# A two-layer attention and conv-FFN decoder on one core: side work of the attention stage placed anew, and four-head score banks lowered by VectorE

## The chip, the core and the metric

The kernel runs on one core of a Trainium2 chip. The metric is the device time of one execution in microseconds. The core has five instruction queues that run beside each other and meet at semaphores: TensorE (PE in the profile), VectorE (DVE), ScalarE (ACT), GpSimd (POOL) and SyncE (SP), which here issues DMAs only. Each queue runs its instructions in the order written; a waiting instruction holds up everything behind it on its engine.

## The reference

A trunk of two layers over 512 tokens of width 1024. In each layer a mixer (8 retention heads, 8 NSA heads in two key groups of four) is followed by a conv FFN, each between RMS norms. What the change touches is in the NSA heads:

```python
def nsa(nq, nkv, ngate, ...):
    kc, vc = compress(kv[0], ...), compress(kv[1], ...)      # 31 compressed keys and values
    def block(b):                                            # 128 queries at a time
        pc = masked_softmax(qb @ kc, mc)                     # compressed branch
        o_cmp = pc @ vc
        kg, vg = ks_blk[.., sel], vs_blk[.., sel]            # all 8 blocks are selected at 512 tokens
        ps = masked_softmax(qb @ kg, causal)                 # selected branch
        pwin = masked_softmax(qb @ kw, window and causal)    # window branch
        return g0 * o_cmp + g1 * (ps @ vg) + g2 * (pwin @ vw)
```

With 512 tokens and 8 blocks of 64 the selection takes every block and the window of 512 is the causal mask, so both branches are plain causal softmaxes over different keys. `masked_softmax` is exp(s - max) over its sum. The retention heads give the first half of the mixer's output `y`, the NSA heads the second; `w_out` multiplies both.

## The kernel before

Nearly all products are done in float32 accuracy from fp32r parts: a tensor `a` is held as `a_hi` (rounded) and `a_lo = a - a_hi`, and a product is three matmuls (hi·hi, hi·lo, lo·hi). Weights stream through a ring of six slots in 110 chunks per layer; ScalarE makes `w_hi` and GpSimd `w_lo`. The order of every engine is written out by hand, engine by engine, with counted semaphores.

The attention stage of a layer, around which the change is made, is a loop over 48 **items** `k`. The 16 **units** (query tile i, key group g, branch b) are softmaxes of 128 queries by 128·(i+1) keys for four heads; each unit has i+1 items, and each pair of units one more item for the compressed branch. For item k the engines do:

- PE: four transposes of the probabilities into a PSUM bank (`turn_p`, L1654; L1648 for the compressed branch), then the product of item k-2 with the values (`product`, L1677 and L1678), then side work by tables: score banks ("jobs") of later units (`SCORES_AT`, L1557 to L1563), one eighth of the last query projection f7 (`Q7_AT`, L1388), the compressed scores of group 1 (`CMP_AT`, L1577, L1583), transposes of the retention output (`turn_y` at `Y_AT`, L1595), and parts of the output projection (`WO_AT`, L1616).
- ACT: the transposed bank to `pt_h` (`p_round`, L839), then the exponentials of the jobs of item k-1 (`exps`, L813), and copies for side work.
- DVE: `pt_l` (`p_rest`, L926), then the minimum of each job's bank (`minima`, L1190; queries are negated, so a minimum is a maximum), and the rests of side work. `turn_p(k)` waits for `p_rest(k-2)` (semaphore `ptl`).
- POOL: the reciprocal of each sum (L603) and the scaling of the probabilities by it and the gate (L609).

A unit of query tile 0 (n = 6, 7, 14, 15) needs only 128 columns per head, so all four heads share one bank: one job, one minimum over four heads (128x4), but four exponentials of 128 columns, each with its own bias and with its sum accumulated. Two projections are spread over this stage too: f6 before the loop, f7 in it. `queries_first(f)` (ACT, two copies, L767) and `queries_rest(f)` (DVE, two instructions, L1135) take the projection out of its bank into `QS`. Bank 7 is shared: the compressed scores of group 0, then f7, then outputs. `compressed_first(g)` (DVE, L1210 to L1214) takes the compressed scores out and counts `c_step` to 3; f7's first matmul waits for that. `y_round(n)` (DVE) takes transposed retention output to `act_hi` (L1199) and `act_lo` (L926).

## Time and profile before

| | us |
|---|---|
| median of 3 runs | 1399.81 (1399.09 to 1399.86) |
| the profiled execution | 1401.01 |
| its span | 1399.1 |
| PE busy | 1363.3 (97%) |
| DVE / POOL / ACT busy | 713.3 (51%) / 700.1 (50%) / 606.3 (43%) |
| mean granted PE clock | 0.99 |

Matmuls are pipelined, so a PE that reads as busy can still be slow: when the granted clock is 0.5, PE is busy all the time and does half the work. The attention loop of layer 0 lies between about 200 and 310 us, that of layer 1 between about 890 and 1000 us.

### The profile page before, as it was taken

How to read it: one execution, taken by the hardware profiler on the slowest of the kernel's cores; microseconds unless marked ns; L12 is line 12 of the kernel's file. 1: busy time of each engine (PE TensorE's matmuls, PEld its weight loads, DVE VectorE, ACT ScalarE, POOL GpSimd, SP SyncE). 2: the span in 40 equal slices, each digit the busy share in tenths (PEclk: the TensorE clock that was granted, in tenths of full speed). 3: DMA queues.
4: the chain of work that ended last, by engine and by line, in shares of the span. 5: the costliest groups of instructions: out<-in, count | busy, mean ns of one | idle time of the engine just before them, and what ended most of it. 6: DMA issues, size and time to landing. Idle time of an engine off the chain costs nothing.

```text
span 1399.1 us, 17721 instructions
## 1 busy us (share of the span) xinstructions
PE 1363.3 (97%) x6904; PEld 1122.8 (80%) x6904; DVE 713.3 (51%) x900; ACT 606.3 (43%) x1087; POOL 700.1 (50%) x544
## 2 busy tenths in 40 slices
PE   8999988999999999999999999989999999999998
PEld 5889866778888888888888887767788888888886
DVE  5406556745544544644462075566355445556443
ACT  4233565756434333433442336656454333343322
POOL 2544775745444444544464456757435444445441
PEclk9999998999999999999999999989999999999999
DMA  5433420022333333333233333100323333333231
GB/s 202 136 100 106 131 65 16 1 91 91 105 91 97 99 93 103 90 103 93 61 121 112 108 106 119 31 16 2 121 68 115 104 91 104 93 96 100 90 106 61
DMA packets 34883, 127.19 MB, mean 91 GB/s; under 512 B 3952, under 2 KB 4464, under 8 KB 34416
## 3 DMA queue, kind: packets, MB, share of 16 engines
q1 hardware_dynamic: 34656, 125.53, 29.2%
q8 instruction: 56, 0.92, 0.3%
q10 hardware_dynamic: 144, 0.52, 0.1%
q14 instruction: 27, 0.22, 0.1%
HBM read 123.94 MB, written 2.10 MB: 90 GB/s over the span
## 4 chain that ended last, share of the span: by engine, by line
PE 89%; ACT 5%; DVE 3%; issue 1%; POOL 1%; DMA 0%; DVEq 0%; POOLq 0%; ACTq 0%; SPq 0%
PE bank L1719 33%; PE bank L1372 17%; PE bank L1751 17%; PE bank L1388 5%; PE bank L1616 3%; PE bank L1654 2%; PE bank L1677 2%; PE bank L1678 1%; ACT E L813 1%; PE bank L1562 1%; PE bank L1563 1%; PE bank L1476 1%; PE bank L1583 1%; PE bank L1340 1%; POOL w_lo L546 1%
## 5 line engine op out<-in xcount | busy, mean ns | idle before, releaser
L546 POOL TENSOR_TENSOR w_lo<-raw,w_hi 128x1024 fp32r<-128x1024 f32 x216 | 521.3, 2419 | 468.4 <-ACT w_hi L643 468.1
L643 ACT ACTIVATE w_hi<-raw 128x1024 fp32r<-128x1024 f32 x220 | 230.9, 1054 | 241.9 <-DMA raw<-wstream 241.8
L1719 PE MATMUL bank<-act_hi,w_hi 128*128 128x512 f32 (+1 forms) x768 | 286.0, 372 | 0.6 <-DVE act_lo L926 0.6
L1719 PE MATMUL bank<-act_hi,w_lo 128*128 128x512 f32 (+1 forms) x768 | 285.2, 371 | 0.0
L1719 PE MATMUL bank<-act_lo,w_hi 128*128 128x512 f32 (+1 forms) x768 | 285.2, 371 | 0.0
L885 ACT ACTIVATE cv<-bank,par 128x512 f32<-128x512 f32 x88 | 68.6, 779 | 286.0 <-PE bank L1719 286.0
L1301 DVE SCALAR_TENSOR_TENSOR cv<-bank,par,cv 128x511 f32<-128x511 f32 x88 | 66.0, 750 | 225.3 <-ACT cv L885 225.3
L1719 PEld LDWEIGHTS bank<-act_hi,w_hi 128*128 128x128 f32 x768 | 144.7, 188 | 26.9 <-DVE act_lo L926 1.6
L1719 PEld LDWEIGHTS bank<-act_hi,w_lo 128*128 128x128 f32 x768 | 144.7, 188 | 25.2
L1719 PEld LDWEIGHTS bank<-act_lo,w_hi 128*128 128x128 f32 x768 | 144.7, 188 | 24.7
L1372 PE MATMUL bank<-w_hi,act_hi 128*128 128x512 f32 (+1 forms) x384 | 144.5, 376 | 0.6 <-DVE w_lo L926 0.5
L1372 PE MATMUL bank<-w_lo,act_hi 128*128 128x512 f32 (+1 forms) x384 | 143.5, 374 | 0.0
L1372 PE MATMUL bank<-w_hi,act_lo 128*128 128x512 f32 (+1 forms) x384 | 143.1, 373 | 0.0
L926 DVE TENSOR_TENSOR act_lo<-gff,act_hi 128x512 fp32r<-128x512 f32 x40 | 92.9, 2334 | 88.0 <-ACT act_hi L896 88.0
L1751 PE MATMUL bank<-w_hi,act_hi 128*128 128x512 f32 x320 | 124.7, 390 | 0.0
L1751 PE MATMUL bank<-w_hi,act_lo 128*128 128x512 f32 x320 | 124.5, 389 | 0.0
L1751 PE MATMUL bank<-w_lo,act_hi 128*128 128x512 f32 x320 | 124.5, 389 | 0.0
L926 DVE TENSOR_TENSOR pt_l<-bank,pt_h 128x512 fp32r<-128x512 f32 (+1 forms) x96 | 65.8, 687 | 76.1 <-ACT pt_h L839 75.8
L1310 DVE TENSOR_TENSOR gff<-cv 128x512 f32<-128x512 f32 x44 | 101.7, 2312 | 4.3 <-ACT cv L891 2.9
L839 ACT ACTIVATE pt_h<-bank 128x512 fp32r<-128x512 f32 (+1 forms) x96 | 56.8, 594 | 78.6 <-PE bank L1678 78.3
L1372 PEld LDWEIGHTS bank<-w_hi,act_hi 128*128 128x128 f32 x384 | 72.1, 188 | 14.4 <-DVE w_lo L926 1.3
L1372 PEld LDWEIGHTS bank<-w_hi,act_lo 128*128 128x128 f32 x384 | 72.2, 188 | 12.6
(175 smaller groups left out, 2231.9 us busy)
## 6 DMA issues: line engine op xcount, KB each, us to landing
raw<-wstream SPq DMA_DIRECT2D x220, 512.0 KB, 3.6
g_all<-gains SPq DMA_DIRECT2D x2, 2048.0 KB, 7.0
x_out<-x SPq DMA_DIRECT2D x8, 256.0 KB, 2.0
x<-x_in SPq DMA_DIRECT2D x3, 512.0 KB, 9.3
const<-consts SPq DMA_DIRECT2D x1, 1030.0 KB, 13.7
g_all<-gains ACTq DMA_DIRECT2D x1, 512.0 KB, 5.1
x<-x_in SPq DMA_DIRECT2D x2, 256.0 KB, 5.2
par<-pars SPq DMA_DIRECT2D x2, 235.0 KB, 3.5
```

The source lines that it names most:

```text
L546: nc.gpsimd.tensor_tensor(w_lo[:, s, :], raw_slot(s), r32(w_hi[:, s, :]), ALU.subtract)\
L643: nc.scalar.activation(w_hi[:, s, :], raw_slot(s), ACT.Copy).then_inc(hi_ready, 1)
L839: nc.scalar.activation(pt_h[0:rows, k % 2, :], bank[0:rows, PT_BANK(k), :], ACT.Copy)\
L885: nc.scalar.activation(cv[:, p, s, :], bank[:, u, :], ACT.Identity, bias=w2[:, col:col + 1, 3], scale=w2[:, col:col + 1, 2])\
L926: return nc.vector.tensor_tensor(out, a, b, ALU.subtract)
L1301: nc.vector.scalar_tensor_tensor(out=y[:, 1:SEQ], in0=u[:, 0:SEQ - 1], scalar=taps[:, col:col + 1, 1], in1=y[:, 1:SEQ], op0=ALU.mult, op1= ...
L1310: nc.vector.tensor_tensor(gff[:, it * 2 + p, :], cv[:, p, 0, :], cv[:, p, 1, :], ALU.mult).then_inc(g_ready, 1)
L1372: last = mm(bank[:, b0 + t, 0:width], a, b, start=(k == 0 and n == 0), stop=(k == KD - 1 and n == 2))
L1388: last = mm(bank[:, F_BANK[f], :], a, v, start=(k == 0 and n == 0), stop=(k == KD - 1 and n == 2))
L1616: last = mm(bank[:, t, :], a, b, start=(k == 0 and n == 0), stop=(k == KD - 1 and n == 2))
L1719: last = mm(bank[:, b, first:end], a, v, start=(k == 0 and n == 0), stop=(k == KD - 1 and n == 2), skip_group_check=True)
L1751: last = mm(bank[:, t + 4 * half, :], a, b, start=(k == 0 and n == 0), stop=(k == TAIL_K[-1] and n == 2))
```

## The change

Three things are done, the same in both layers.

1. The compressed scores of group 0 go one projection step earlier (steps 11 to 14 in place of 12 to 15), and `compressed_first(0)` stands behind the minimum of job 13 in place of after the loop. f6 leaves its bank at item 1 in place of inside the early loop; f7 runs at items 0 to 6 (in place of 1 to 8) and leaves its bank at item 7 (in place of 9). `turn_y` goes to items 8, 11, 14, 17, its first waits for f6 only (`q_l` 6 in place of 8), and its `act_hi` copy goes from DVE to ACT. Jobs, the group-1 compressed scores, two chunk splits and the output projection move by one to three items.
2. For the four units with one bank (`LOWERED`), DVE subtracts the minimum from the bank into `E`, ACT takes one exponential of 128x512 in place, and DVE sums it (`sums`, two items behind the job).
3. POOL's reciprocal of these units waits for `summed` in place of `e_done`.

The diff (lines of context cut):

```diff
@@ -290,6 +290,7 @@
+        UNITS = [(i, g, b) for g in range(NKV) for i in reversed(range(T)) for b in range(2)]
@@ -307,6 +308,9 @@
         e_done = sem("e_done", G * NU)
+        LOWERED = [n for n in range(NU) if UNITS[n][0] == 0]
+        lowered = sem("lowered", len(LOWERED))
+        summed = sem("summed", len(LOWERED))
@@ -333,19 +337,19 @@
         HALF_0_FIRST, HALF_0 = (0, 3, 2, 1), (3, 2, 1, 0)
-        CMP_BANK, CMP_AT = (7, 0), (0, 22)
-        Q7_AT = 1
-        Y_AT = (9, 11, 13, 15)
-        WO_AT = {24: [(0, 0)], 26: [(0, 1)], 28: [(3, 0)], 31: [(3, 1)], 36: [(2, 0)], 37: [(2, 1)], 38: [(3, 2)],
-         39: [(3, 3)], 41: [(1, 0)], 43: [(1, 1)], 44: [(2, 2)], 47: [(2, 3)]}
+        CMP_BANK, CMP_AT = (7, 0), (0, 24)
+        Q7_AT = {0: (0, 1), 1: (1, 3), 2: (3, 4), 3: (4, 5), 4: (5, 6), 5: (6, 7), 6: (7, KD)}
+        Q6_END, Q7_END = 1, 7
+        Y_AT = (8, 11, 14, 17)
+        WO_AT = {27: [(0, 0)], 28: [(0, 1)], 31: [(3, 0)], 32: [(3, 1)], 38: [(2, 0)], 39: [(2, 1)], 40: [(3, 2)],
+         41: [(3, 3)], 42: [(1, 0)], 43: [(1, 1)], 44: [(2, 2)], 47: [(2, 3)]}
...
-        WO_CHUNK_AT = {1: C_WO + 1, 8: C_WO + 2, 17: C_WO + 3, 27: C_WO + 4, 33: C_WO + 5}
...
-
-        UNITS = [(i, g, b) for g in range(NKV) for i in reversed(range(T)) for b in range(2)]
+        WO_CHUNK_AT = {3: C_WO + 1, 10: C_WO + 2, 17: C_WO + 3, 27: C_WO + 4, 33: C_WO + 5}
@@ -374,8 +378,8 @@
-        UNIT_SCORES = {4: (3, 4), 5: (5, 6), 6: (7,), 7: (10,), 8: (11, 12, 13, 14), 9: (15, 16, 17, 18),
-               10: (19, 20, 21, 22), 11: (23, 24, 25, 26), 12: (28, 30), 13: (32, 34), 14: (36,), 15: (38,)}
+        UNIT_SCORES = {4: (3, 4), 5: (5, 6), 6: (7,), 7: (10,), 8: (12, 13, 14, 16), 9: (17, 18, 19, 20),
+               10: (21, 22, 23, 24), 11: (25, 26, 27, 28), 12: (29, 31), 13: (33, 35), 14: (37,), 15: (39,)}
@@ -599,7 +603,10 @@
                 pool.wait_ge(p_scaled, upto(p_scaled, l, scaled_through(n - SB, 2 * p + 1)))
-            pool.wait_ge(e_done, upto(e_done, l, EXP_NO[n, 2 * p + 1]))
+            if n in LOWERED:
+                pool.wait_ge(summed, upto(summed, l, LOWERED.index(n) + 1))
+            else:
+                pool.wait_ge(e_done, upto(e_done, l, EXP_NO[n, 2 * p + 1]))
@@ -801,6 +808,11 @@
             width = P * (UNITS[n][0] + 1)
+            if n in LOWERED:
+                act.wait_ge(lowered, upto(lowered, l, LOWERED.index(n) + 1))
+                e = E[:, slot, :, col:col + width]
+                nc.scalar.activation(e, e, ACT.Exp, scale=-1.0).then_inc(e_done, G)
+                return
@@ -813,6 +825,11 @@
+
+        def y_round(n):
+            act.wait_ge(y_turned, upto(y_turned, l, n + 1))
+            nc.scalar.activation(act_hi[:, 0:4, n * P:(n + 1) * P],
+                                 bank[:, 0, :].rearrange("p (k c) -> p k c", k=4), ACT.Copy).then_inc(y_h, 1)
@@ -826,8 +843,6 @@
                 hi(l, C_WO)
-            if z == 13:
-                queries_first(6)
@@ -862,8 +877,12 @@
                 exps(z)
-            if k == Q7_AT + 8:
+            if k == Q6_END:
+                queries_first(6)
+            if k == Q7_END:
                 queries_first(7)
+            if k in Y_AT:
+                y_round(Y_AT.index(k))
@@ -1191,13 +1210,26 @@
                 .then_inc(m_step, 1)
+            if n in LOWERED:
+                slot, col = E_AT[n]
+                dve.wait_ge(m_step, upto(m_step, l, z + 1))
+                dve.wait_ge(pt_done, upto(pt_done, l, last_turn(E_AFTER[n]) + 1))
+                nc.vector.tensor_tensor(E[:, slot, :, col:col + width],
+                                        bank[:, S_BANK(z), :].rearrange("p (q c) -> p q c", q=G),
+                                        s_bias[:, n % SB, :].unsqueeze(2).broadcast_to([P, G, width]),
+                                        ALU.subtract).then_inc(lowered, 1)
+
+        def sums(n):
+            slot, col = E_AT[n]
+            dve.wait_ge(e_done, upto(e_done, l, EXP_NO[n, G - 1]))
+            if n >= SB:
+                dve.wait_ge(rec_done, upto(rec_done, l, PAIR_NO[n - SB, 1] + 1))
+            nc.vector.tensor_reduce(out=s_sum[:, n % SB, :], in_=E[:, slot, :, col:col + P], axis=AXX,
+                                    op=ALU.add).then_inc(summed, 1)
...
-        def y_round(n):
-            dve.wait_ge(y_turned, upto(y_turned, l, n + 1))
-            nc.vector.tensor_copy(act_hi[:, 0:4, n * P:(n + 1) * P],
-                                  bank[:, 0, :].rearrange("p (k c) -> p k c", k=4)).then_inc(y_h, 1)
+        def y_rest(n):
@@ -1222,9 +1254,8 @@
                 compressed_values_rest()
-            if z == 14:
-                queries_rest(6)
-        compressed_first(0)
+            if z == 13:
+                compressed_first(0)
@@ -1275,10 +1306,15 @@
                 minima(z)
-            if k == Q7_AT + 8:
+            for z in jobs_at(k - 2):
+                if JOBS[z][0] in LOWERED:
+                    sums(JOBS[z][0])
+            if k == Q6_END:
+                queries_rest(6)
+            if k == Q7_END:
...
             if k - 1 in Y_AT:
-                y_round(Y_AT.index(k - 1))
+                y_rest(Y_AT.index(k - 1))
@@ -1588,7 +1624,7 @@
                 pe.wait_ge(y_step, upto(y_step, l, 8))
-                pe.wait_ge(q_l, upto(q_l, l, 8))
+                pe.wait_ge(q_l, upto(q_l, l, 6))
@@ -1631,8 +1667,8 @@
                 second_layer()
-            if n >= 12:
-                compressed_scores(0, n - 12)
+            if 11 <= n < 15:
+                compressed_scores(0, n - 11)
@@ -1683,10 +1719,10 @@
                 job_scores(z)
-            if Q7_AT <= k < Q7_AT + KD:
-                if k == Q7_AT:
+            if k in Q7_AT:
+                if k == min(Q7_AT):
                     pe.wait_ge(c_step, upto(c_step, l, 3))
-                feature_tile(l, 7, range(k - Q7_AT, k - Q7_AT + 1))
+                feature_tile(l, 7, range(*Q7_AT[k]))
```

On **VectorE**, just ahead of the attention loop of layer 0. `s_bias<-bank` is the minimum of a score bank, `c_stat` and `cE<-bank` are `compressed_first(0)`, `QS` is `queries_rest(6)`, `pt_l` belongs to items 0 to 2. Before:

```order
L1190 TENSOR_REDUCE s_bias<-bank 128x1 [waits s_done] x6
L1135 SCALAR_TENSOR_TENSOR QS<-bank,QS 64x512 [waits q_h]
L1135 SCALAR_TENSOR_TENSOR QS<-bank,QS 64x512
L1190 TENSOR_REDUCE s_bias<-bank 128x1 [waits s_done]
L1210 TENSOR_REDUCE c_stat<-bank 128x16 [waits cs_done]
L1212 TENSOR_SCALAR c_stat<-c_stat 128x16 [waits c_step]
L1214 TENSOR_TENSOR cE<-bank,c_stat 128x512 [waits c_step]
L926 TENSOR_TENSOR pt_l<-bank,pt_h 128x512 [waits pth] x3
```

After:

```order
L1209 TENSOR_REDUCE s_bias<-bank 128x1 [waits s_done] x5
L1242 TENSOR_REDUCE c_stat<-bank 128x16 [waits cs_done]
L1244 TENSOR_SCALAR c_stat<-c_stat 128x16 [waits c_step]
L1246 TENSOR_TENSOR cE<-bank,c_stat 128x512 [waits c_step]
L1209 TENSOR_REDUCE s_bias<-bank 128x1 [waits s_done] x2
L945 TENSOR_TENSOR pt_l<-bank,pt_h 128x512 [waits pth] x2
L1154 SCALAR_TENSOR_TENSOR QS<-bank,QS 64x512 [waits q_h]
L1154 SCALAR_TENSOR_TENSOR QS<-bank,QS 64x512
L945 TENSOR_TENSOR pt_l<-bank,pt_h 128x512 [waits pth]
```

The compressed scores' three instructions now stand ahead of two minima and of f6's rest, and f6's rest stands behind the `pt_l` of items 0 and 1.

On **ScalarE**, around items 7 to 10 of layer 0. `E,s_sum` are exponentials with their sums, `E<-E` the new single exponential, `QS` is `queries_first(7)`, `act_hi<-bank` the moved copy of `turn_y`, `w_hi` a weight chunk. Before:

```order
L839 ACTIVATE pt_h<-bank 32x512 [waits pv_done,pt_done]
L813 ACTIVATE E,s_sum<-bank,s_bias 128x128 [waits pt_done,m_step]
L813 ACTIVATE E,s_sum<-bank,s_bias 128x128 x3
L839 ACTIVATE pt_h<-bank 128x512 [waits pv_done,pt_done]
L767 ACTIVATE QS<-bank 64x512 [waits w_used]
L767 ACTIVATE QS<-bank 64x512
L839 ACTIVATE pt_h<-bank 128x512 [waits pv_done,pt_done] x2
L813 ACTIVATE E,s_sum<-bank,s_bias 128x128 [waits pt_done,m_step]
L813 ACTIVATE E,s_sum<-bank,s_bias 128x128 x3
L846 ACTIVATE o_a<-bank 64x512 [waits pv_done]
```

After:

```order
L774 ACTIVATE QS<-bank 64x512 [waits w_used]
L774 ACTIVATE QS<-bank 64x512
L854 ACTIVATE pt_h<-bank 32x512 [waits pv_done,pt_done]
L814 ACTIVATE E<-E 128x4x128 [waits lowered]
L831 ACTIVATE act_hi<-bank 128x4x128 [waits y_turned]
L650 ACTIVATE w_hi<-raw 128x1024 [waits raw_loaded2]
L854 ACTIVATE pt_h<-bank 128x512 [waits pv_done,pt_done] x3
L814 ACTIVATE E<-E 128x4x128 [waits lowered]
L831 ACTIVATE act_hi<-bank 128x4x128 [waits y_turned]
L861 ACTIVATE o_a<-bank 64x512 [waits pv_done]
```

f7's copies now stand ahead of the `pt_h` of item 8; four exponentials have become one, which waits for `lowered`; and two `act_hi` copies have joined the queue.

On **VectorE**, items 7 to 11 of layer 0 (`QS` is `queries_rest(7)`, `E<-bank` the lowering, `s_sum<-E` the sum, `act_lo` the rest of `turn_y`). Before:

```order
L1190 TENSOR_REDUCE s_bias<-bank 128x4 [waits s_done]
L926 TENSOR_TENSOR pt_l<-bank,pt_h 32x512 [waits pth]
L926 TENSOR_TENSOR pt_l<-bank,pt_h 128x512 [waits pth]
L1135 SCALAR_TENSOR_TENSOR QS<-bank,QS 64x512 [waits q_h]
L1135 SCALAR_TENSOR_TENSOR QS<-bank,QS 64x512
L926 TENSOR_TENSOR pt_l<-bank,pt_h 128x512 [waits pth]
L1190 TENSOR_REDUCE s_bias<-bank 128x4 [waits s_done]
L1199 CAST act_hi<-bank 128x4x128 [waits y_turned]
L926 TENSOR_TENSOR act_lo<-bank,act_hi 128x4x128 [waits y_h]
```

After:

```order
L1209 TENSOR_REDUCE s_bias<-bank 128x4 [waits s_done]
L1217 TENSOR_TENSOR E<-bank,s_bias 128x4x128 [waits pt_done,m_step]
L1154 SCALAR_TENSOR_TENSOR QS<-bank,QS 64x512 [waits q_h]
L1154 SCALAR_TENSOR_TENSOR QS<-bank,QS 64x512
L945 TENSOR_TENSOR pt_l<-bank,pt_h 32x512 [waits pth]
L945 TENSOR_TENSOR pt_l<-bank,pt_h 128x512 [waits pth]
L1227 TENSOR_REDUCE s_sum<-E 128x4 [waits e_done]
L945 TENSOR_TENSOR act_lo<-bank,act_hi 128x4x128 [waits y_h]
L945 TENSOR_TENSOR pt_l<-bank,pt_h 128x512 [waits pth]
L1209 TENSOR_REDUCE s_bias<-bank 128x4 [waits s_done]
L1217 TENSOR_TENSOR E<-bank,s_bias 128x4x128 [waits pt_done,m_step]
L945 TENSOR_TENSOR pt_l<-bank,pt_h 128x512 [waits pth]
```

f7's rest has moved from behind the `pt_l` of item 9 to ahead of that of item 8, the cast is gone, and each four-head minimum has a lowering behind it and a sum two items later.

## Rows read from the trace of the kernel before

**Rows 1.** The page's first part: busy time, share, instructions.

```profile
PE 1363.3 (97%) x6904; PEld 1122.8 (80%) x6904; DVE 713.3 (51%) x900; ACT 606.3 (43%) x1087; POOL 700.1 (50%) x544
```

**Rows 2.** Waits of PE, 180 to 330 us: total, times, longest.

```profile
PE bank L1595 <- DVE QS L1135: 3.6, 1, 3.6
PE bank L1595 <- DVE act_lo L926: 2.2, 2, 2.0
PE bank L1388 <- DVE cE L1214: 2.2, 1, 2.2
```

**Rows 3.** The same view, 870 to 1020 us.

```profile
PE bank L1595 <- DVE act_lo L926: 2.6, 2, 1.3
```

**Rows 4.** Windows: length, busy PE PEld DVE ACT POOL, PEclk, DMA share, GB/s.

```profile
206.00:209.40 3.40, 3.40 (x13) 2.39 (x11) 1.28 (x2) 0.60 (x1) 3.40 (x2) 0.51 0.02 5
...
226.50:233.30 6.80, 6.80 (x26) 5.21 (x26) 2.64 (x4) 0.80 (x2) 0.67 (x2) 0.51 0.00 0
...
916.00:926.20 10.20, 9.85 (x37) 7.99 (x38) 4.20 (x8) 3.06 (x11) 2.25 (x5) 0.50 0.01 2
933.00:936.40 3.40, 2.09 (x15) 1.39 (x15) 3.07 (x6) 2.20 (x4) 1.72 (x3) 1.00 0.00 0
```

**Rows 5.** Timeline, the wait at 201 us: start, length, instruction, idle before.

```profile
203.07 0.69 DVE L1214 TENSOR_TENSOR cE<-bank,c_stat 128x512 f32<-128x512 f32 x1
...
203.82 0.50 PE L1388 MATMUL bank<-act_hi,w_hi 128*128 128x512 f32 x1 [2.17 <-DVE cE L1214]
```

**Rows 6.** Timeline, the wait at 223 us.

```profile
221.58 0.34 ACT L813 ACTIVATE E<-bank,s_bias 128x128 f32<-128x128 f32 x1
...
223.43 1.19 ACT L767 ACTIVATE QS<-bank 64x512 fp32r<-64x512 f32 x2
...
224.64 1.41 DVE L1135 SCALAR_TENSOR_TENSOR QS<-bank,QS 64x512 fp32r<-64x512 f32 x2 [0.40 <-ACT QS L767]
...
226.20 0.94 PE L1595 MATMUL bank<-const,qr 128*128 128x128 f32 x4 [3.61 <-DVE QS L1135]
```

**Rows 7.** Timeline, the wait at 237 us.

```profile
237.71 0.68 DVE L1199 CAST act_hi<-bank 128x512 fp32r<-128x512 f32 x1
...
239.18 0.66 PE L1595 MATMUL bank<-const,qr 128*128 128x128 f32 x4 [1.99 <-DVE act_lo L926]
```

**Rows 8.** Groups by form: busy, mean ns of one, idle before.

```profile
L926 DVE TENSOR_TENSOR pt_l<-bank,pt_h 128x512 fp32r<-128x512 f32 x80 | 55.0, 689 | 60.6 <-ACT pt_h L839 60.2
...
L839 ACT ACTIVATE pt_h<-bank 128x512 fp32r<-128x512 f32 x80 | 47.4, 595 | 64.6 <-PE bank L1678 64.3
...
L813 ACT ACTIVATE E<-bank,s_bias 128x256 f32<-128x256 f32 x32 | 14.9, 475 | 0.7 <-DVE s_bias L1190 0.7
...
L1243 DVE TENSOR_TENSOR o_f<-bank,o_a 64x256 f32<-64x256 f32 x32 | 13.7, 427 | 6.6 <-ACT o_a L846 3.0 <-POOL act_lo L616 2.7
...
L1214 DVE TENSOR_TENSOR cE<-bank,c_stat 128x512 f32<-128x512 f32 x4 | 2.8, 692 | 0.1
...
L1253 DVE TENSOR_REDUCE c_rec<-cE 128x16 f32<-128x512 f32 x4 | 2.7, 676 | 0.0
...
L862 ACT ACTIVATE cE<-cE 128x512 f32<-128x512 f32 x4 | 2.5, 634 | 1.7 <-DVE cE L1214 1.7
```

**Rows 9.** Timeline of PE, items 4 and 7 at full clock.

```profile
210.58 0.60 PE L1654 MATMUL bank<-const,E 128*128 128x128 f32 x4
...
211.49 0.28 PE L1557 MATMUL bank<-causal_b,ident_b 128*128 128x256 bf16 x1
...
212.08 0.39 PE L1388 MATMUL bank<-act_hi,w_hi 128*128 128x512 f32 x1
...
218.11 0.39 PE L1557 MATMUL bank<-causal_b,ident_b 128*128 128x512 bf16 x1
...
219.18 0.44 PE L1388 MATMUL bank<-act_hi,w_hi 128*128 128x512 f32 x1
```

## The prediction

> **What bounds the kernel now.** I read the page's first part first. PE is busy for 97% of the span and no other engine for more than 51% [rows 1]: the reader is to see that only what PE waits for, or what slows it, can be won. Then the waits of PE in the two attention stages, the only place the change touches. Three waits stand out in layer 0: 3.6 us for the rest of f7's queries, 2.2 for the rests of the retention output (2.0 of it at once), 2.2 for the compressed scores of group 0 [rows 2], 8.0 us in sum. Layer 1 repeats the first and the third of these rows to the tenth, and its second is 2.6 [rows 3]: 8.4 us. Then the windows, for the clock. After each wait comes a stretch at 0.5 of full clock (1.2 in place of 2.4 GHz) in which PE reads as busy: 3.4 us at 206, 6.8 us at 226.5, 10.2 us at 916 [rows 4]; the 3.4 us pattern stands once more in layer 0 (at 240.1) and once in layer 1 (at 895.5), 13.6 us in each layer. At half clock half the work is done, so each layer loses 6.8 us, since PE is busy for nearly all of these stretches. All in all 8.0 + 8.4 + 6.8 + 6.8 = 30.0 us are what the placing of side work costs.
>
> Last I read the timeline of each wait. At 201 us PE has transposed items 0 and 1 and wants f7's first matmul, which stands behind VectorE's `cE` [rows 5]. At 223 us PE stands at the first `turn_y`, which waits for f7's rest: ScalarE had four exponentials (0.34 each, from 221.58), a `pt_h`, then the two copies (1.19), then VectorE 1.41, then PE 3.61 us late [rows 6]. At 237 us VectorE makes `act_hi` (0.68), then `act_lo`, then PE's next transposes come 1.99 late [rows 7].
>
> **The change, part by part.** *f7 and the compressed scores.* The scores of group 0 end one step sooner, and VectorE takes them out ahead of f6's rest (1.41, as f7's in [rows 6]) and of two minima. I place `c_step` 3 at about 200.8, some 3.0 us sooner than the 203.76 at which `cE` ends now [rows 5], when PE still has its first transposes to do. The wait of 2.2 us goes, in both layers. What is late next is the `pt_l` of item 0, behind job 15's exponential: I leave 0.1 us for it. Gain 2.1 a layer, and the 3.4 us at half clock behind it, 1.7.
>
> *f7's rest and `turn_y`.* The first `turn_y` now needs f6 alone, which is out six items earlier; the 3.6 us wait goes, and its half clock with it (6.8 in layer 0, 10.2 in layer 1, so 3.4 and 5.1). But f7's copies still stand in the in-order queues, now ahead of the `pt_h` and the `pt_l` of item 8, for which the transposes of item 10 wait. From the end of the product in item 7: ScalarE has `pt_h` 0.6, two exponentials of 128x256 at 0.48 [rows 8], f7's copies 1.2; VectorE then f7's rest 1.4 [rows 6] and `pt_l` 0.7 [rows 8]: 4.9 us. PE meanwhile has the four-head bank, 219.18 - 218.11 = 1.1 [rows 9], the transposes and products of items 8 and 9 at 211.49 - 210.58 = 0.9 each, and the four transposes of `turn_y`, about 0.4: 3.3 us. So a new wait of 1.6 us at item 10. Bounds: 0, if the copies meet an idle ScalarE, and 3.6, the wait that it replaces; I take 1.6.
>
> *`turn_y`'s copy to ScalarE.* It takes 0.68 off VectorE [rows 7] and puts a copy like `pt_h`'s, 0.6, on ScalarE [rows 8]. The rests are used three items later in place of two, so the 2.2 (2.6) us wait goes, with its 3.4 us at half clock in layer 0.
>
> *The lowering.* A unit loses four exponentials at 0.34 [rows 6], 1.4 us of ScalarE, and gets one like L862, 0.63. VectorE gets a subtraction like L1214, 0.69, and a sum like L1253, 0.68 [rows 8]. Over four units VectorE gains 5.5 us of work and loses 2.7 of casts; ScalarE loses 3.1 and gets 2.4. Nothing of this is on PE's path by itself. What it does is put a new wait in ScalarE's queue: the exponential of unit 7 waits for `lowered`, and behind it stand `turn_y`'s copy, `o_a` and the `pt_h` of item 12. For the two late units (14, 15) the sums come at items 39 and 41 and their transposes at 45 and 46, with output-projection matmuls between; GpSimd's two reciprocals and four scalings hide there, at no cost. If that cover were gone, a unit's 0.69 + 0.68 would show, 1.4 us.
>
> *VectorE in items 9 to 18.* With the waits gone PE asks faster, and VectorE is next. I count for it: 10 `pt_l` at 0.69, 7 minima and 2 sums at 0.68, one lowering 0.69, 4 `act_lo` at 0.69, four `o_f` additions at 0.43 [rows 8] = 18.2 us, or 16.2 if each of the 28 overlaps the next by 0.07, an estimate. PE has 10 items at 0.9, the four-head bank 1.1, 6 jobs at 212.08 - 211.49 = 0.6 [rows 9], 3 `turn_y` at 0.4: 14.9. The difference is 1.3 to 3.3 us of new short waits at items 12 to 17, plus hand-overs to ScalarE and back; I take 2.6. Bounds: 0 and 5.
>
> *Item 24.* `compressed_first(1)`, about 1.6 us of VectorE (a reduction and a subtraction as in [rows 8], and a small instruction), had output-projection matmuls in items 24 and 26 beside it. They now start at 27. I take 0.9, between 0 and 1.6.
>
> *The clock.* Around item 10 there is one wait of 1.6 us with short ones behind it. A stretch of 3.4 us with PE busy for only 2.09 is still granted full clock (the last of [rows 4]), so I don't charge a drop in each layer, but one of 3.4 us in one of them: 1.7.
>
> Here stands what the Trainium skill says against this change, in TensorE: Matmul & The Clock Gate, section A second HAM failure mode: psum-queue depth-cycling: a PE that idles for a moment between groups often enough goes back and forth between its two clock levels, and the re-warming eats the throughput. By that rule many short waits are no better than three long ones; the last of [rows 4] speaks against it, and it is the third case below.
>
> *Sum.* Won: 30.0. Given back: 2 × (0.1 + 1.6 + 2.6 + 0.9) + 1.7 = 12.1. Net 17.9. The profiled execution took 1401.0 (span 1399.1 and 1.9 around it), so 1383.1 against itself. It lies 1.2 above the median of the runs; against the median it is **1382 us**.
>
> **The rivals.** *All of it comes (A).* ScalarE and VectorE keep up: the copies of f7 meet a free ScalarE and the hand-overs overlap, leaving 2 us in all. Then 1399.8 - 28 = 1372. For it: VectorE is busy only half of the span [rows 1]. Against it: the count above, in which VectorE has more than PE.
>
> *The short waits keep the clock down (C).* After item 10 PE stays at half clock for 6.8 us in each layer, as it did after 226.5. Half of that, 3.4 us a layer less the 1.7 charged, adds 5.1, and slower transposes lengthen VectorE's round trips by perhaps 2: 1382 + 7 = 1389. For it: the half stretch at 916 is 10.2 us long although PE is busy in it [rows 4]. Against it: the last row there.
>
> *The change doesn't reach the clock (D).* If the half stretches came from the kind of work and not from the waits, only 16.4 - 2 × 5.2 = 6 us would be won: 1394. Against it: each half stretch follows a wait of 2 us or more.
>
> *Slower (E).* The mechanism: VectorE's and ScalarE's queues now wait for each other by turns at each four-head bank (minimum, lowering, exponential, sum), and every item from 9 to 20 waits for a full round trip: `pt_h` 0.6, `pt_l` 0.7, transposes and product 0.9, and 0.69 + 0.63 + 0.68 on top in a few. That decides from 15 us of new waits a layer, 1.3 an item over 12 items; at 1.4 an item the time is 1403. Against it: only two such banks lie in that stretch.
>
> **How the numbers follow.** The forecast at 1382 (1376 to 1387) has 0.50, A 0.17, C 0.21, D 0.07, E 0.05. The range that holds 8 in 10 takes in the first and C and reaches towards A: 1374 to 1392, left out are most of A and D, and E. 0.2% of the time, about what a measurement of this kernel can tell from no change, is 2.8 us. Faster is all but E and a sliver of D: 0.93. E and that sliver lie about half within 0.2% of the time before: the same 0.04, slower 0.03.
>
> **What would show it.** In the new trace the waits on `QS` by `turn_y`, on `cE` by f7 and on `act_lo` by `turn_y` are gone or under 0.5 us each. PE waits for `pt_l` instead, about 1.6 us at item 10 (near 218 us) and in short pieces to item 17, about 4 us a layer. The half-clock stretches fall from 27.2 us to under 7. Four E exponentials of 128x128 per unit are gone, one of 128x512 near 0.63 stands in place. PE's busy work at full clock is the same. I am wrong if a wait on `turn_y` or `cE` of over 1 us stays, if the half-clock time is over 14 us, or if the waits on `pt_l` come to under 1 us or over 8 us a layer.

## The result, and the profile after

The changed kernel takes **1379.18 us** (median of 4 runs, 1378.21 to 1380.65), the kernel before 1399.84 beside it: a ratio of 0.9854, 95% interval 0.9837 to 0.9871, so 20.7 us faster. The forecast was 1382, range 1374 to 1392. Two executions of the experiments below, of 6355 and 7727 us, were disturbed and are left out. The profiled execution is the quickest of the four, 1378.2 (span 1376.4): 22.7 us under the span before. That splits into 12.0 of PE's busy time and 10.7 of its idle time (35.8 before, 25.1 after), from the page's first part, which answers to [rows 1]:

```profile
span 1376.4 us, 17693 instructions
...
PE 1351.3 (98%) x6904; PEld 1113.3 (81%) x6904; DVE 725.5 (53%) x908; ACT 603.2 (44%) x1039; POOL 698.8 (51%) x544
```

PE has the same 6904 matmuls in less busy time: that part is the clock. The waits of PE from 180 to 302 us, answering to [rows 2]:

```profile
PE bank L1690 <- DVE pt_l L945: 3.6, 4, 1.6
PE bank L1593 <- ACT E L825: 0.6, 1, 0.6
PE bank L1593 <- DVE QS L1154: 0.5, 1, 0.5
PE bank L1684 <- DVE pt_l L945: 0.4, 1, 0.4
```

None of the three old waits is left; waits on `pt_l` have come, 3.6 us in four pieces (3.8 in five in layer 1, where 860 to 985 us otherwise reads the same). The first and largest stands at item 10. The timeline of the ACT, DVE and PE instructions that lead to it:

```profile
216.64 1.20 ACT L774 ACTIVATE QS<-bank 64x512 fp32r<-64x512 f32 x2
...
217.86 0.59 ACT L854 ACTIVATE pt_h<-bank 32x512 fp32r<-32x512 f32 x1
...
217.92 1.41 DVE L1154 SCALAR_TENSOR_TENSOR QS<-bank,QS 64x512 fp32r<-64x512 f32 x2
...
219.36 0.68 DVE L945 TENSOR_TENSOR pt_l<-bank,pt_h 32x512 fp32r<-32x512 f32 x1
...
220.09 0.66 PE L1690 MATMUL bank<-const,E 128*128 128x128 f32 x4 [1.62 <-DVE pt_l L945]
```

Read it from below: PE gets the `pt_l` of item 8, which stood behind f7's rest (two instructions, 1.41), which waited for f7's copies (1.20). The second piece is at item 14:

```profile
224.80 0.63 ACT L814 ACTIVATE E<-E 128x512 f32<-128x512 f32 x1 [0.61 <-DVE E L1217]
...
225.34 0.58 ACT L831 ACTIVATE act_hi<-bank 128x512 fp32r<-128x512 f32 x1
...
225.81 0.58 ACT L861 ACTIVATE o_a<-bank 64x512 f32<-64x512 f32 x1
...
226.42 0.89 DVE L1274 TENSOR_TENSOR o_f<-bank,o_a 64x256 f32<-64x256 f32 x2 [1.12 <-ACT o_a L861]
...
227.34 0.69 DVE L945 TENSOR_TENSOR pt_l<-bank,pt_h 128x512 fp32r<-128x512 f32 x1
...
228.09 0.66 PE L1690 MATMUL bank<-const,E 128*128 128x128 f32 x4 [1.02 <-DVE pt_l L945]
```

Here VectorE is idle for 1.12 us: the lowered exponential of unit 7, itself 0.61 late behind VectorE's subtraction, and `turn_y`'s copy stand ahead of `o_a`. The third is at item 26, behind `compressed_first(1)`:

```profile
251.01 0.68 DVE L1242 TENSOR_REDUCE c_stat<-bank 128x16 f32<-128x512 f32 x1
...
252.11 0.69 DVE L1246 TENSOR_TENSOR cE<-bank,c_stat 128x512 f32<-128x512 f32 x1
...
253.92 0.66 PE L1690 MATMUL bank<-const,E 128*128 128x128 f32 x4 [0.71 <-DVE pt_l L945]
```

The windows around the largest waits of both layers, answering to [rows 4] (busy time of each engine, then granted clock, DMA share, GB/s), show full clock, as do all windows of both attention stages:

```profile
216.00:219.40 3.40, 2.47 (x19) 1.86 (x17) 3.27 (x6) 3.35 (x10) 2.86 (x5) 1.00 0.26 101
219.40:222.80 3.40, 2.71 (x20) 2.15 (x20) 2.54 (x5) 2.06 (x4) 0.53 (x1) 1.00 0.00 0
...
226.20:229.60 3.40, 2.38 (x14) 1.33 (x12) 3.11 (x6) 2.51 (x7) 2.06 (x2) 1.00 0.00 0
899.10:902.50 3.40, 3.40 (x23) 2.71 (x24) 2.60 (x5) 1.37 (x3) 1.13 (x2) 1.00 0.00 0
```

The new instructions of the lowering, by group (line, tile, count, busy us, mean ns), against [rows 8]:

```profile
L1217 DVE TENSOR_TENSOR E<-bank,s_bias 128x512 f32<-128x512 f32 x4 | 2.8, 691 | 0.1
...
L1227 DVE TENSOR_REDUCE s_sum<-E 128x4 f32<-128x512 f32 x4 | 2.7, 676 | 0.0
L814 ACT ACTIVATE E<-E 128x512 f32<-128x512 f32 x4 | 2.5, 625 | 1.1 <-DVE E L1217 1.1
```

### The profile page after: what moved, and what is told of

Read it like the earlier page. It is cut to its first block, busy times and chain, and to the rows that moved or that the text cites. A ratio compares the mean times of both kernels' runs of the same rounds, so it can differ in the third digit from the quotient of the medians.

```text
span 1376.4 us, 17693 instructions
## 1 busy us (share of the span) xinstructions
PE 1351.3 (98%) x6904; PEld 1113.3 (81%) x6904; DVE 725.5 (53%) x908; ACT 603.2 (44%) x1039; POOL 698.8 (51%) x544
## 4 chain that ended last, share of the span: by engine, by line
PE 87%; ACT 5%; DVE 4%; issue 2%; POOL 1%; DMA 0%; DVEq 0%; POOLq 0%; ACTq 0%; SPq 0%
PE bank L1755 33%; PE bank L1408 17%; PE bank L1787 17%; PE bank L1424 5%; PE bank L1652 3%; PE bank L1690 2%; ACT E L825 1%; PE bank L1713 1%; PE bank L1512 1%; PE bank L1714 1%; DVE pt_l L945 1%; PE bank L1619 1%; PE bank L1598 1%; PE bank L1376 1%; DVE s_bias L1209 1%
## 5 line engine op out<-in xcount | busy, mean ns | idle before, releaser
L1408 PEld LDWEIGHTS bank<-w_lo,act_hi 128*128 128x128 f32 x384 | 72.1, 188 | 12.2
```

Of the source, the lines that this page charges most:

```text
L1408: last = mm(bank[:, b0 + t, 0:width], a, b, start=(k == 0 and n == 0), stop=(k == KD - 1 and n == 2))
```

## The experiments

Each was timed in 5 rounds beside the kernel before. The table gives the ratio to it and, from the profiled execution, PE's waits of over 1 us in layer 0's attention stage and the time at half clock in both stages together (granted clock read over both stages in steps of 0.85 us, and added up). The kernel before had medians of 1399.84 to 1401.02 us in the four groups of runs, so ratios are compared between groups and not times. The columns of waits and half clock stand for one execution each. They leave out what lies outside the two stages: in eight of the fourteen profiled executions there are 3.4 us at half clock near 9 us (6.8 in "+ f6 at item 1"), in the first work of the kernel, which is the same in all of them.

| kernel | ratio (95%) | waits over 1 us, layer 0 | half clock |
|---|---|---|---|
| before | 1 | 2.2, 3.6, 2.0 | 27.4 |
| changed | 0.9854 (0.9837 to 0.9871) | 1.6, 1.0 | 0 |
| placing only | 0.9845 (0.9832 to 0.9859) | 1.6, 1.4 | 0 |
| lowering only | 1.0014 (1.0005 to 1.0023) | 2.2, 3.6, 1.9, 1.3 | 30.8 |
| `turn_y` early | 0.9917 (0.9904 to 0.9931) | 2.2, 1.3, 1.3, 1.3 | 3.4 |
| scores early | 1.0014 (1.0005 to 1.0023) | 3.7, 3.6, 1.3, 1.3 | 23.9 |
| + f6 at item 1 | 0.9990 (0.9981 to 0.9999) | 2.3, 3.6, 1.8, 1.3 | 20.4 |
| + chunk at item 3 | 0.9948 (0.9935 to 0.9962) | 1.3, 3.6, 1.8, 1.3 | 17.0 |
| + f7 from item 0 | 0.9944 (0.9932 to 0.9957) | 4.3, 1.7, 1.3 | 13.6 |
| changed, `turn_y` waits | 0.9882 (0.9868 to 0.9895) | 2.3, 1.0 | 10.2 |
| changed, y copy on DVE | 0.9870 (0.9855 to 0.9884) | 1.6 | 10.2 |
| changed, rest behind `pt_l` | 0.9867 (0.9852 to 0.9883) | 1.0 | 0 |
| all behind | 0.9847 (0.9834 to 0.9861) | 1.0 | 0 |
| chunk at item 12 | 0.9839 (0.9825 to 0.9852) | none | 6.8 |

**Placing only.** `LOWERED = []`, all else as changed.

> The changed kernel with the four-head banks as before (no LOWERED unit: four exponentials with their own bias and sum, no subtraction and no sum on VectorE); all placing and turn_y's copy on ScalarE stay. Theory (the gain comes from the placing alone): within 1.5 us of the changed kernel's 1379.2. Read closer: ScalarE has 0.7 us more behind pt_h of item 8, so the pt_h of item 9, which is ready at once in the changed kernel, comes late by up to 1 us, and against that the wait of 1.0 us at item 14 falls by half, since nothing waits for a subtraction: 1379.7. Rival (the lowering carries part of it, as relief of ScalarE): 1384 or more.

1379.36, the changed kernel's time: the placing is the whole gain. The chain at item 14 got longer, not shorter (1.37 for 1.02): unit 7's four exponentials run from 225.12 to 226.5 ahead of `turn_y`'s copy and `o_a`, and VectorE is idle for 1.71 ahead of `o_f` where it was 1.12.

**Lowering only.** The kernel before with the subtraction, the exponential and `sums`.

> The kernel before with the lowering alone (subtraction and sum on VectorE, one exponential), all tables as before. Theory (placing alone): the three waits stay, only the 3.6 us wait for f7's rest shrinks, by up to 0.7 a layer, because ScalarE's four exponentials of unit 6 ahead of f7's copies become one: 1398.4 to 1399.8, half-clock stretches as before. Rival (the lowering carries part): under 1395.

1403.1, slower by 0.14%. The first half of the theory failed: the 3.6 us wait did not shrink. The timeline of ScalarE ahead of it tells why:

```profile
221.43 0.61 ACT L813 ACTIVATE E<-E 128x512 f32<-128x512 f32 x1
222.54 0.60 ACT L850 ACTIVATE pt_h<-bank 128x512 fp32r<-128x512 f32 x1 [0.50 <-PE bank L1708]
223.03 1.20 ACT L773 ACTIVATE QS<-bank 64x512 fp32r<-64x512 f32 x2
```

ScalarE now waits 0.50 for PE's product ahead of `pt_h`, so the time saved in the exponentials is idle time there. VectorE's extra work comes out at the later `turn_y` in layer 0 (3.2 us on `act_lo` for 2.2), but PE's idle time over the whole span is nearly as before (36.1 us for 35.8). Of the 2.7 us that the profiled execution is longer 2.4 are PE's busy time, which goes with more half clock: 30.8 us for 27.4 in the stages, and 3.4 at the start. So a cost of the lowering on this placing is not shown apart from the clock.

**`turn_y` early.** One number in the kernel before:

```diff
                     if n == 0:
                         pe.wait_ge(y_step, upto(y_step, l, 8))
-                        pe.wait_ge(q_l, upto(q_l, l, 8))
+                        pe.wait_ge(q_l, upto(q_l, l, 6))
```

> The kernel before with one number changed: the first turn_y waits for q_l 6 in place of 8. Theory (a half-clock stretch is there because of the wait ahead of it): the 3.6 us wait goes in both layers, and with it 6.8 and 10.2 us at half clock, which is 7.2 + 3.4 + 5.1 = 15.7; f7's copies now stand ahead of the probabilities and give a new wait of some 2 us at items 11 or 12: 1388, with the half-clock time down from 27 to about 10 us or, if the new wait counts like the others (2 us), about 17 us and 1391. Rival (the half clock comes with the kind of work in items 9 to 20): only the waits go, 1396, half-clock time near 27 us.

1389.17, and in the profiled execution half clock falls from 27.4 to 3.4 us, further than the 10 or 17 expected: in place of one new wait of 2 us there are three of 1.3, and the wait of 2.0 is gone too. (Three of the five runs show a mean clock of 0.994 for its 0.997, so they had more half clock; where is not known.) The kind and order of PE's work is the same, so the half clock hung on the waits: D falls in its strong form. But not on each of them alike. The wait of 2.17 for `cE` stands in both layers, and only the second is followed by half clock (windows behind it):

```profile
205.20:208.60 3.40, 3.03 (x19) 2.21 (x18) 2.10 (x4) 1.48 (x3) 3.40 (x3) 1.00 0.03 5
...
889.30:892.70 3.40, 3.40 (x12) 2.38 (x11) 1.28 (x2) 0.60 (x1) 3.40 (x2) 0.51 0.02 5
```

**Scores early**, then three more steps on top of it: the four parts of the change that stand ahead of PE's first long wait.

```diff
-                    if n >= 12:
-                        compressed_scores(0, n - 12)
+                    if 11 <= n < 15:
+                        compressed_scores(0, n - 11)
...
+                    if z == 13:
+                        compressed_first(0)
                     if z == 14:
                         queries_rest(6)
-                compressed_first(0)
```

> The kernel before with the compressed scores of group 0 one projection step earlier and their outputs taken out behind the minimum of job 13, f6 and f7 placed as before. Theory: the wait of 2.2 us for cE goes in both layers and 3.4 us at half clock behind it: 2 x (2.1 + 1.7) = 7.6, so 1392.2. Rival (the clock does not follow this wait): 1395.6. Rival (VectorE only hands the delay on to f6's rest and the first pt_l): 1399.

No gain (1402.1): the wait left f7 and came back, larger, at the transposes of item 2.

```profile
199.87 1.22 ACT L767 ACTIVATE QS<-bank 64x512 fp32r<-64x512 f32 x2 [0.32 <-PE bank L1389]
...
201.20 1.41 DVE L1135 SCALAR_TENSOR_TENSOR QS<-bank,QS 64x512 fp32r<-64x512 f32 x2
...
203.80 1.04 ACT L643 ACTIVATE w_hi<-raw 128x1024 fp32r<-128x1024 f32 x1
...
204.75 1.07 ACT L839 ACTIVATE pt_h<-bank 128x512 fp32r<-128x512 f32 x2
...
206.12 1.12 PE L1655 MATMUL bank<-const,E 128*128 128x128 f32 x4 [3.75 <-DVE pt_l L926]
```

The second rival was right: f6's copies and rest and, on ScalarE, a weight chunk's `w_hi` still stand ahead of the first `pt_h`. So f6 was moved too (`queries_first(6)` and `queries_rest(6)` to item 1):

> The kernel before with two things done: the compressed scores of group 0 one step earlier, as in the run of the scores alone, and f6's way out of its bank moved from the early loop to item 1. f7 and turn_y as before. Theory after the run of the scores alone (there the wait only moved from cE to the pt_l of item 0, because f6's rest and the minima still stood ahead of it on VectorE): only the two moves together take the wait of 2.2 away; 2 x (2.1 + 1.7) = 7.6 less than before, some 1392 to 1393, and PE waits under 0.6 us before item 3. Rival (f6's copies and rest at item 1 now hold up the pt_l of items 1 and 2): a wait of over 1.5 us at item 3, and no gain.

The wait is 2.28 (under 0.6 was expected), the time 0.1% under before: the moves together are still not enough. Its timeline gives the rest of the bill:

```profile
203.18 1.05 ACT L643 ACTIVATE w_hi<-raw 128x1024 fp32r<-128x1024 f32 x1
...
204.12 1.08 ACT L837 ACTIVATE pt_h<-bank 128x512 fp32r<-128x512 f32 x2
...
205.49 0.66 PE L1655 MATMUL bank<-const,E 128*128 128x128 f32 x4 [2.28 <-DVE pt_l L926]
```

Then the chunk (`WO_CHUNK_AT = {3: ...` for `1:`), then f7 with its table at items 0 to 6:

> The kernel with the scores and f6 moved, and besides the first weight chunk's split moved from item 1 to item 3 (on ScalarE it stood, 1.05 us, ahead of the pt_h of item 0). Theory (the wait of 2.28 for the pt_l of item 0 that was left there is made of three pieces: 1.05 of w_hi, two steps of f7 that PE does not yet have, 2 x 0.64, and nothing else): the wait is 1.2 us in both layers, 1398 or, if the half-clock stretch behind it goes too, 1394. Rival (the chunk is not on this chain, or comes late somewhere else): the wait stays at 2.3, no change.

> The same with f7 at items 0 to 6, as in the changed kernel, f7's way out still at item 9. Theory: the last 1.28 us of the first wait are covered by f7's steps, so no wait of over 0.3 us before item 9, and no half clock before it; 2 x (2.2 + 1.7) = 7.8 less than before, 1392.5. The 3.6 us wait of the first turn_y stays, with its half clock. Rival (f7's exit was what mattered and its start is worth nothing): over 1396.

```profile
204.38 0.66 PE L1655 MATMUL bank<-const,E 128*128 128x128 f32 x4 [1.34 <-DVE pt_l L926]
```
```profile
223.02 0.64 PE L1596 MATMUL bank<-const,qr 128*128 128x128 f32 x4 [4.31 <-DVE QS L1135]
```

2.28 less 0.94 is 1.34 with the chunk moved (the first of the two rows), and with f7's two steps it is gone; the ratio is 0.9944, 7.8 us, the sum that was reckoned for this wait and its half clock. Its parts are others: in the profiled execution PE's idle time fell by only 3.0 us, for the 4.4 reckoned, and half clock in the stages by 13.8, twice the 6.8 that stand behind this wait before. Most of the gain came with the chunk: no half clock follows the wait of 1.34 any more. f7's earlier start, with its way out held at item 9, adds 0.7 to the next wait (second row).

**Changed, `turn_y` waits** (`q_l` 8 in place of 6):

> The changed kernel with one number changed: the first turn_y waits for q_l 8 again (f7's rest, which is at item 7 now). PE then waits about 2.3 us in one piece ahead of turn_y at item 8, and no more for the pt_l of item 8 (1.6). Theory 1 (a wait of over 2 us in the attention stage is followed by half clock, one of 1.6 is not): 0.8 us a layer more of waiting and 3.4 to 6.8 us at half clock in each layer, 1384 to 1387. Theory 2 (in the changed kernel nothing brings the clock down, whatever a single wait is): 1380.8 and no half-clock stretch.

1383.64. One wait of 2.35 for one of 1.62, and half clock in both layers of the profiled execution, 3.4 and 6.8 us: theory 1 as to the long wait, and the mix of work of the changed kernel does not protect it. By the times alone it is not clear, since the two intervals just meet. That a wait of 1.6 stays without half clock doesn't hold in the next run.

```profile
219.50:222.90 3.40, 3.20 (x13) 2.93 (x14) 0.73 (x2) 1.85 (x3) 0.00 (x0) 0.51 0.00 0
901.90:905.30 3.40, 3.40 (x14) 2.08 (x11) 1.52 (x3) 2.25 (x4) 0.15 (x1) 0.54 0.00 0
```

**Changed, y copy on VectorE:**

> The changed kernel with turn_y's act_hi copy back on VectorE (four per layer, 0.68 each) in place of ScalarE (0.58). Theory (at item 14 the chain goes over ScalarE: exponential 0.63, this copy 0.58, o_a, then o_f and pt_l on VectorE): that wait falls from 1.0 to about 0.5, and VectorE's copies give short waits of some 0.5 elsewhere: within 1 us of the changed kernel, 1379. Rival (VectorE is the fuller one in items 9 to 18, as the prediction counted): 0.68 for three copies a layer come out as waits on pt_l, 1383.

1382.2; its interval and the changed kernel's overlap. The time lies near the rival's, but not for its reason: the waits are as the theory had them (that of item 14 is gone, 0.4 twice elsewhere), and half clock came, 6.8 and 3.4 us behind the old waits of 1.64 and 1.62. This is the slowest of its four executions (1385.93). It has two more stretches of 3.4 us, one near 10 us and one at 805 us, behind a wait of 1.70 for VectorE's `gate` in the retention stage, of which the next run tells. The other three show clocks of 0.998 to 0.994, much like the changed kernel's, so it is not shown that the moved copy brings half clock. The very wait of 1.62 that the changed kernel takes in layer 1 at full clock (above, 899.10) is here followed by this:

```profile
907.10:910.50 3.40, 3.40 (x18) 3.10 (x17) 3.31 (x6) 0.76 (x2) 2.98 (x6) 0.57 0.00 0
```

**Three ways to better the changed kernel.** First f7's rest on VectorE behind the `pt_l` of item 8:

```diff
                     if k < NI:
                         p_rest(k)
+                    if k == Q7_END + 1:
+                        queries_rest(7)
```

> The changed kernel with f7's rest on VectorE (two instructions, 1.41 us) moved from item 7 to behind the pt_l of item 8; ScalarE's copies stay where they are. Theory (the 1.6 us wait at item 10 is the chain pt_h, exponentials, f7's copies, f7's rest, pt_l): the pt_l of item 8 then starts right behind its pt_h, 0.9 us sooner, so the wait is 0.7 a layer, and half of what is won may be lost at item 11: 1377.4 to 1378.3. Rival (the next pt_l takes over the whole delay): 1379.2, a new wait of 0.9 at item 11.

The wait at item 10 is 0.74, as reckoned, but the time is 1381.2 (1377.4 to 1378.3 was expected; the interval overlaps the changed kernel's), and 1380.2 in the profiled execution. That one has a new wait of 1.54 far away, in layer 1's retention stage:

```profile
797.64 0.16 DVE L1049 TENSOR_SCALAR gate<-gate 128x24 f32<-128x24 f32 x1
...
798.01 2.35 POOL L550 TENSOR_TENSOR w_lo<-raw,w_hi 128x1024 fp32r<-128x1024 f32 x1 [1.06 <-ACT w_hi L650]
798.06 2.34 DVE L1049 TENSOR_SCALAR gate<-gate 128x24 f32<-128x24 f32 x1
...
800.54 1.16 PE L1487 MATMUL bank<-qT,kT 64*128 64x128 f32 x16 [1.54 <-DVE gate L1049]
```

A VectorE instruction of 0.16 us takes 2.34 when it starts behind a GpSimd one that runs to 800.36. In the changed kernel it started at 797.19, 0.5 before GpSimd's, and took 0.16. The other three runs show clocks of 0.995 and 0.994 for this one's 0.999; why they take 1.0 to 1.7 us longer still, no trace tells.

Then f7's copies behind `pt_h` of item 8 as well, `o_a` ahead of the exponentials, and the chunk of item 10 at 13 (its `w_hi` is made an item sooner); last the same with that chunk at 12:

> The changed kernel with f7's copies on ScalarE and its rest on VectorE both behind the pt_h and the pt_l of item 8, the split of a weight chunk (1.04 us of ScalarE at item 9) moved to item 12, and o_a taken out ahead of the exponentials and turn_y's copy in its item. Theory: no wait at item 10, a part of it (0.5 to 1) given back at item 11 because the copies, the exponential and turn_y's copy stand ahead of pt_h of item 9; the wait of 1.0 at item 14 falls to about 0.5: 1.2 to 1.6 us a layer less than changed, 1376 to 1377. Rival (ScalarE is simply full in items 8 to 12, and any order gives the same sum): 1379.

> The kernel with everything of f7's way out behind pt_h and pt_l of item 8 and o_a ahead, its weight chunk's split now at item 11 on ScalarE (in a gap of 1.5 us there) in place of item 12, where its 1.05 us stood ahead of the pt_h of item 12. Theory: the wait at item 14 falls from 1.05 to about 0.5 in each layer, 1377.6. Rival (the wait at item 14 is the round trip o_a, o_f, pt_l on VectorE, whatever ScalarE does): 1378.6, as with the chunk at item 12.

```profile
221.41 0.66 PE L1690 MATMUL bank<-const,E 128*128 128x128 f32 x4 [0.39 <-DVE pt_l L945]
...
225.58 1.05 ACT L650 ACTIVATE w_hi<-raw 128x1024 fp32r<-128x1024 f32 x1
...
227.89 0.66 PE L1690 MATMUL bank<-const,E 128*128 128x128 f32 x4 [1.05 <-DVE pt_l L945]
```

In the first the wait at item 10 gives way to 0.39 at item 11, and that at item 14 stays, now because of the chunk (1378.6, where 1376 to 1377 was expected). In the second it is gone too: 1.8 us on `pt_l` in the whole stage for 3.6. So the rival of the last run (a round trip on VectorE, whatever ScalarE does) is out, though the median of its four times, 1378.7, lies at the rival's 1378.6. Its four runs go from 1376.4 to 1380.1 with granted clocks of 0.999 to 0.995, and the profiled one has half clock in layer 1 with hardly a wait ahead of it (0.21 us at most in 20 us):

```profile
917.00:920.40 3.40, 3.33 (x25) 2.39 (x22) 3.31 (x7) 2.38 (x6) 2.35 (x4) 1.00 0.00 0
920.40:923.80 3.40, 3.40 (x26) 2.87 (x25) 1.99 (x5) 2.28 (x7) 3.19 (x6) 1.00 0.01 2
924.20:927.60 3.40, 3.40 (x17) 2.74 (x16) 1.57 (x4) 1.56 (x5) 0.26 (x1) 0.52 0.00 0
```

Both have a median ratio below the changed kernel's, but the intervals overlap: no version here is shown to beat it.

## Why the prediction was right, point by point

- **The waits that go.** All three went in both layers. The step for `cE` ended right (7.8 us measured for 7.6), in part by luck as told above, and I had put it down to the scores alone. In the order in which they were added, scores, f6 and chunk each leave a wait, and only f7's start takes the last of it. In "what is late next" I had left 0.1 for the first `pt_l`; it is not late only because the other three were moved as well. The wait on `act_lo` I had put beside the copy's move to ScalarE; with the copy back on VectorE it stays at 0.4 and 0.5, so it is not the copy that took it away. The wider spacing of `turn_y` is what is left, and was not run alone.
- **The new wait at item 10**: 1.6 forecast, 1.62 measured, by the chain that was forecast (`pt_h`, exponentials, f7's copies, f7's rest, `pt_l`).
- **VectorE in items 12 to 17**: 2.6 a layer forecast, 1.02 at item 14 and little else measured. This is the term that was most mis-sized. I had laid VectorE's busy sum against PE's and added hand-overs, and PE's sum was 2 us short. In the trace the 28 instructions of VectorE are as counted and take 16.6 us in layer 0 (220.90 to 240.82), near my 16.2; but PE, from the transposes of item 9 (217.40) to those of item 19 (237.32), is busy for 16.9 where I had counted 14.9. So VectorE was not the fuller engine. What PE waits for at item 14 is an order (exponential, copy, `o_a`). Item 24: 0.9 forecast, 0.71 at item 26 measured.
- **Idle time in sum.** 6.0 us net was forecast (16.4 won, 10.4 given back). It fell by 10.7. Of the 4.7 more, 3.2 are the term of items 12 to 17 (2 x 2.6 less 2 x 1.02). Most of the rest are small waits that I had not counted as won: GpSimd's `act_lo`, 0.5 a layer, and 0.4 a layer of `pt_l` ahead of item 2, from the same view as [rows 2]:

```profile
PE bank L1654 <- DVE pt_l L926: 0.6, 2, 0.4
...
PE bank L1616 <- POOL act_lo L616: 0.5, 1, 0.5
```

- **The clock.** Won 13.6, given back 1.7: 11.9, and PE's busy time fell by 12.0. The agreement is luck. The profiled execution paid no half clock in the stages, and so should have shown 13.6: a stretch at half clock cost 0.44 of its length here (12.0 of 27.4), not half; why is open. The other three runs show granted clocks of 0.998, 0.996 and 0.995 for its 0.999 and take 0.9 to 2.4 us longer. Whether that is the 1.7 is not shown: the profiled execution of placing only, also at 0.998 and 1379.36 us, has full clock in both stages and its 3.4 us of half clock near 9 us, outside the change. I had also written that a stretch comes after each wait; layer 1's two waits of 1.3 [rows 3] have none.
- **The lowering**: priced at nothing on PE's path, and measured so (placing only: the same time). Alone, on the old placing, the kernel is 0.14% slower, nearly all of it clock in the profiled execution.
- **The rivals.** A (1372): 1.6 + 1.0 + 0.7 = 3.3 us a layer came back where it had 1, so no. E is out. D fell with one number changed, though the one drop without a wait leaves it a part. C, for which the Trainium skill stood (TensorE: Matmul & The Clock Gate, A second HAM failure mode: psum-queue depth-cycling), did not come in the changed kernel's profiled execution: short waits of 1.6 and 1.0 at full clock. But the run with the y copy on VectorE shows its pattern, 10.2 us at half clock in the stages with no wait there over 1.64, so C is not ruled out for every execution.

The whole is 22.8 us against the profiled execution where 17.9 was forecast, 20.7 against 17.8 by the medians.

## What to carry to other kernels

When a wait is taken away, walk each in-order queue from the old releaser to the next thing that the waiting engine needs: here three pieces of side work stood between (scores, f6, a weight chunk); the first two that were moved bought 0.1%, and most of the gain came with the third. Price an engine that looks full by the order of its instructions around the wait, and not by its busy sum alone. In these traces a wait of over 2 us on TensorE nearly always cost some 1.5 us or more on top in clock (an estimate, 3.4 us at 0.44), one of 1.3 never, so take the long ones first.

## What the runs showed of the hardware

**The clock is not a function of the last wait.** In the attention stages of all these traces 25 waits of PE were of 2.17 us and more; 24 had 3.4 to 10.2 us at half clock (1.2 of 2.4 GHz) setting in during them or just behind, and one had none (2.17, layer 0 of the one-number run). Of 15 waits from 1.58 to 1.99 four had it, and of those around 1.3 none. Waits of 1.62 were followed by none in the changed kernel and by 3.4 us in the one with the y copy on VectorE. One drop, at 924 us in the last windows above, had no wait of over 0.21 us in the 20 us before it. What sets it off there stays open. Another drop, near 9 us, comes in eight of the fourteen profiled executions and not in the rest. Runs of one kernel differ by the clock (granted clock 0.999 to 0.995, 1376.4 to 1380.1 us), so a gain of 1 us in the waits can't be told from the clock's luck in these four or five runs.

**A small VectorE instruction can wait for GpSimd.** 0.16 us became 2.34, ending 0.04 after GpSimd's subtraction. It is no single case: in the run with the y copy on VectorE the same instruction takes 2.23 behind a GpSimd one (801.16, and 801.00 to 803.36). In the changed kernel an earlier one of these takes 1.77, again to 0.04 behind GpSimd's end, where PE doesn't wait for it:

```profile
793.70 2.38 POOL L550 TENSOR_TENSOR w_lo<-raw,w_hi 128x1024 fp32r<-128x1024 f32 x1 [0.97 <-ACT w_hi L650]
794.35 1.77 DVE L1049 TENSOR_SCALAR gate<-gate 128x24 f32<-128x24 f32 x1
```

The Trainium skill tells of this in SBUF — State Buffer, Who interferes with whom: a tensor_scalar of VectorE can need the port pair that it shares with GpSimd, and whichever starts first keeps it for its whole instruction. The traces agree. It makes the time of a distant stage depend on half a microsecond of phase, which is more than some of the gains that were sought here.
